# Sample's score items laid over fewer slots of the projection, and six small loads moved from its slot 293 to its slot 287

## What is computed

```python
h = rms_norm(x, ln_w)
proj = einsum('bsd,de->bse', h, w_in)         # 1024 -> 8720 columns: q, k, v of 24 heads, gates, the recurrence's q, k, v
# branch A, three groups of 8 heads, windows 128 / 512 / 2048 with dilation 1 / 4 / 16
s = where(band, q @ k.T, -inf); p = softmax(s); o = p @ v; lse = m + log(den)
o_attn = sum_g softmax_g(lse) * o_g
# branch B, gated linear attention, chunks of 64 (prompt) or 8 (sample)
o_gla, state = gla_recurrence(gq, gk, gv, log_a, s0, chunk)
y = rms_norm(x + (sigmoid(mg_a) * (o_attn * silu(az)) @ w_attn_out
                + sigmoid(mg_b) * (rms_norm(o_gla) * silu(gz)) @ w_gla_out) @ w_out)
```

## Time and profile before

| | us |
|---|---|
| median of 3 runs | 2485.26 (2484.94 to 2485.51) |
| the profiled execution | 2486.58 |
| its span, first to last instruction | 2484.8 |
| TensorE busy in it | 2450.7 (99%) |
| VectorE busy | 1214.5 (49%) |
| ScalarE busy | 908.1 (37%) |
| GpSimd busy | 199.1 (8%) |
| mean granted TensorE clock | 0.996 of full |

### The profile page before, as it was taken

How to read it: one execution, slowest core, us unless ns; L and a number is a source line. 1 busy time by engine, 2 the same in 40 slices (tenths; PEclk the granted TensorE clock), 3 DMA queues, 4 the chain that set the end, 5 groups by cost and what they waited for, 6 DMA issues and landing times.

```text
span 2484.8 us, 37018 instructions
## 1 busy us (share of the span) xinstructions
PE 2450.7 (99%) x13710; PEld 1969.5 (79%) x13710; DVE 1214.5 (49%) x2860; ACT 908.1 (37%) x2163; POOL 199.1 (8%) x367
## 2 busy tenths in 40 slices
PE   9999999999999999999999999999999998999998
PEld 6888887887778888887888888788778755888887
DVE  5323422333321115565666666556756447656663
ACT  5224534443332214223544544445424233212221
POOL 0000000000000000112111111222222100000000
PEclk9999999999999999999999999999999999999999
DMA  6333323332323223457667666797777799444341
GB/s 192 103 121 114 105 91 125 103 100 90 112 96 102 93 91 117 144 170 240 209 220 224 202 204 204 215 296 216 206 230 215 219 338 346 172 161 151 140 167 68
DMA packets 209122, 416.97 MB, mean 168 GB/s; under 512 B 32513, under 2 KB 53521, under 8 KB 206833
## 3 DMA queue, kind: packets, MB, share of 16 engines
q1 hardware_dynamic: 166912, 293.60, 35.5%
q0 software_dynamic: 29712, 95.06, 13.1%
q10 hardware_dynamic: 12320, 25.96, 2.8%
HBM read 313.33 MB, written 112.99 MB: 172 GB/s over the span
## 4 chain that ended last, share of the span: by engine, by line
PE 93%; DMA 3%; DVE 2%; ACT 1%; issue 1%; SPq 0%; POOL 0%; DVEq 0%; ACTq 0%
PE b_acc L1231 20%; PE b_acc L1233 19%; PE b_acc L1232 19%; PE c_p_s L1281 3%; PE c_p_o L1304 3%; PE c_p_t L1292 3%; PE c_p_qk L1268 3%; PE f_p_b L2002 2%; PE f_p_b L2004 2%; PE f_p_b L2003 2%; PE f_p_z L2002 2%; PE f_p_z L2004 2%; PE f_p_z L2003 2%; PE b_acc L1237 2%; PE b_acc L1238 1%; PE e_p_o L1923 1%
## 5 line engine op out<-in xcount | busy, mean ns | idle before, releaser
L1231 PE MATMUL b_acc<-b_whi,hT_hi 128*128 128x512 f32 x2048 | 819.9, 400 | 3.9 <-DVE b_wlo L967 1.5
L1233 PE MATMUL b_acc<-b_whi,hT_lo 128*128 128x512 f32 x2048 | 799.5, 390 | 0.0
L1232 PE MATMUL b_acc<-b_wlo,hT_hi 128*128 128x512 f32 x2048 | 798.6, 390 | 0.0
L1231 PEld LDWEIGHTS b_acc<-b_whi,hT_hi 128*128 128x128 f32 x2048 | 384.4, 188 | 101.2 <-issue 9.8
L1233 PEld LDWEIGHTS b_acc<-b_whi,hT_lo 128*128 128x128 f32 x2048 | 384.5, 188 | 82.4
L1232 PEld LDWEIGHTS b_acc<-b_wlo,hT_hi 128*128 128x128 f32 x2048 | 385.1, 188 | 73.4
L967 DVE SCALAR_TENSOR_TENSOR b_wlo<-b_raw,a_lnw,b_whi 128x512 fp32r<-128x512 f32 x268 | 192.7, 748 | 365.3 <-ACT b_whi L759 364.9
L773 ACT COPY b_stage<-b_acc 128x512 f32<-128x512 f32 (+2 forms) x198 | 115.3, 582 | 539.6 <-PE b_acc L1233 529.4
L797 ACT ACTIVATE c_sm<-c_sm,c_ends 128x256 f32<-128x256 f32 (+1 forms) x384 | 172.8, 451 | 129.9 <-DVE c_ends L1052 129.8
L759 ACT ACTIVATE b_whi<-b_raw,a_lnw 128x512 fp32r<-128x512 f32 x268 | 182.9, 714 | 3.9 <-ACT c_og L815 1.4
L771 ACT ACTIVATE b_stage<-b_acc 128x512 f32<-128x512 f32 x96 | 57.4, 598 | 307.7 <-PE b_acc L1233 307.3
(11 more groups left out here) (320 smaller groups left out, 3091.2 us busy)
## 6 DMA issues: line engine op xcount, KB each, us to landing
b_raw<-in_w_in SPq DMA_DIRECT2D x134, 512.0 KB, 4.3
tm<-b_stage SPq DMA_DIRECT2D x256, 256.0 KB, 2.1
a_x<-tm POOLq DMA_DIRECT2D x192, 256.0 KB, 4.9
b_ck<-in_cache_kv_w POOLq DMA_DIRECT2D x104, 256.0 KB, 5.0
c_qk<-tm SPq DMA_DIRECT2D x101, 256.0 KB, 3.6
f_m<-tm SPq DMA_DIRECT2D x16, 1024.0 KB, 5.8
c_v<-tm SPq DMA_DIRECT2D x53, 256.0 KB, 4.3
og<-c_og ACTq DMA_DIRECT2D x48, 264.0 KB, 3.9
```

The costliest lines, as they stand in the source:

```text
L1231: nc.tensor.matmul(out, stat_hi, mov_hi, start=(k == 0), stop=False)
L1232: nc.tensor.matmul(out, stat_hi, mov_lo, start=False, stop=False)
L1233: return nc.tensor.matmul(out, stat_lo, mov_hi, start=False, stop=(k == KC - 1))
```

## The change

Two lines. In `project`, the items are laid over the slots from begin + 3 to four slots ahead of the last turn's first, instead of six slots ahead of the projection's end: the last item stands in slot 281 instead of 287. In `finish`, SyncE's wait for all scores and the six small loads behind it move from t = 6 to t = 0 of `tile`, from slot 293 to slot 287.

```diff
@@ project
     begin = turns[len(CHUNKS[0])].first
-    item_at = [begin + 3 + m * (NSLOT - 6 - begin - 3) // N_IT for m in range(N_IT)]
+    item_at = [begin + 3 + m * (turns[-1].first - 4 - begin - 3) // N_IT for m in range(N_IT)]
@@ finish, sync, tile(t)
-            if t == TPH - 2:
+            if t == 0:
                 sp.wait_ge(over.scored, over.scores)
                 load_vn(1)
                 sp.dma_start(diag[:, :], A["dec_diag"]).then_inc(gw_in, 16)
                 sp.dma_start(gw[:, :], A["gla_norm_w"].rearrange("a (p b) -> p (a b)", b=1)).then_inc(gw_in, 16)
                 sp.dma_start(g_v[:, :], TMs[SEQ:TOK, TM_GV * CH:(TM_GV + 1) * CH]).then_inc(gw_in, 16)
```

## The result

| | before | after |
|---|---|---|
| median, runs side by side on one chip | 2485.26 us | 2493.25 us |
| lowest to highest | 2483.09 to 2486.06 | 2490.56 to 2494.40 |
| after over before | | 1.0036 [1.0027, 1.0046] |
| span of the profiled execution | 2484.8 us | 2490.8 us |
| mean granted TensorE clock | 0.996 | 0.993 |

The change makes the kernel slower: by 8.0 us between the medians, by 0.36% in the ratio, whose interval lies clear of 1. Forecast were 2484.2 us and a range of 2481.5 to 2488.0. One execution of a kernel further down (the squeezed items) took 6604.77 us, why isn't known, and is left out of that kernel's numbers.

The account below looks back on a forecast made before the run. It took TensorE's matmuls to bound the kernel before 1976 us and the transfer queue from there to 2086 us. Terms 0 + 0 - 1.1 us gave 2484.2 us, from the 2485.26 us median; range 2481.5 to 2488.0.

Parts of the forecast that it names:

- part 1: Score items laid over slots 159 to 281 instead of 159 to 287: cost or gain 0.
- Denser items also mean denser loads: VectorE's waits for score loads, 15.1 us in all, grow five per cent, hidden under matmuls: 0, bounds 0 and +3.9 us.
- the 1.9 us for c_qk: Longest of three TensorE waits from 990 to 1979 us said possibly to concern the change; no term given.
- VectorE's two waits of 1.3 us: TensorE's waits at slot 253's SiLU product and slot 258's recurrence tile: first goes, second grows equally; 0, bounds -2.6 and +2.6.
- rival (d): Faster: both 1.3 us waits go and all 1.4 us of moved loads arrive: -4.0 us, 2481.3 us; chance 0.12.
- Both signs of being wrong: Between 990 and 1979 us, TensorE shows a new wait on VectorE or a new stretch at half clock.
- (b): Last turn: six loads delay the mask up to 1.4 us, TensorE's softmax wait brings half clock: 2489.0 us; chance 0.09.
- (c): Slots 246 to 261: a score-load wait up to 3.9 us reaches TensorE, half clock behind: +6.2, 2491.5 us; chance 0.09.
- Part 2: Six small loads moved to slot 287 fit SyncE's idle 3.7 us, delay nothing, and free the full DMA stretch: -1.1 us.
- The -1.1 us: Gain at V and weight loads after the move, 0.3 us lost to engines running dry; bounds -1.4 and 0.
- the 1.4: Time of all 16 DMA engines for the six loads' 0.49 MB at 353 GB/s, taken out of the full stretch.
- rival (a): The moved loads were hidden anyway, so their 1.4 us is lost where SyncE waits for buffers: 2485.3 us; chance 0.18.

Follow-up runs that it names:

- the squeezed items: The changed kernel with items up to slot 261 placed as before and the last 43 squeezed into slots 262 to 281: 2492.59 us, ratio 1.0027.
- the items alone: The changed kernel with the wait for the scores and the six small loads back in slot 293, items over slots 159 to 281: 2491.84 us, ratio 1.0027.
- GpSimd held back: The changed kernel, with GpSimd waiting for d_glr to land before it issues the loads of item 165: 2486.40 us, ratio 1.0009.
- the loads alone: The kernel before with only the score wait and six small loads moved to slot 287, items where they were: 2483.76 us, ratio 0.9993.
- the 1 MB copy: The kernel before plus a 1 MB memory-to-memory copy issued by SyncE in slot 251, ahead of the recurrence's loads: 2489.44 us, ratio 1.0021.
- the two with both holes: The changed kernel without items in slots 180 to 182 and 250 to 252: 2482.81 us; the same with the small loads back in slot 293: 2485.62 us.
- before with both holes: The kernel before (last item in slot 287, small loads in 293) without items in slots 180 to 182 and 250 to 252: 2489.76 us, ratio 1.0023.
- hole at 180: The changed kernel with no score item in slots 180 to 182 only: 2490.67 us, ratio 1.0028.
- hole at 250: The changed kernel with no score item in slots 250 to 252 only: 2493.30 us, ratio 1.0041.

## Why the prediction was wrong

**The step that failed** is the last paragraph of part 1, "Denser items also mean denser loads", taken at 0. It asked only what a score load does to VectorE, which waits for it, and bounded that by VectorE's waits. It did not ask what the score loads do to the other transfers that are under way. In fact VectorE's waits for them fell (8.6 us in 9 waits, against 15.1 in 11), and the bill came at two of SyncE's loads, for which TensorE waits: 3.9 us at c_qk and 5.9 us at d_glr, wait and half clock together, where the sum had 0. The rows for it were at hand: the 1.9 us for c_qk was named as a wait "that could have to do with this change", and then no step took it up. GpSimd's queue around slots 182 and 252 had to be laid beside SyncE's, item by item by the formula of `item_at`; its gap of 10.13 us ahead of 1738.43 shows how much luck the old list had there.

**Counting items per slot** hid it. 1.67 or 1.76 a slot is a mean; the change shifts the phase of the whole list. The comparison slot by slot was made for VectorE's work at slots 252 to 257, not for the loads, which run up to three items ahead.

**VectorE's two waits of 1.3 us**, sum 0, make -0.7 us in all, within the bounds, but not by the step that was given. The wait for slot 253's product went, as the item count said. The one at the tile of slot 258 was to grow to some 2.6 us; it went too, which was the sign of rival (d). Two others came: 0.5 us for the product of slot 255 and 1.4 us at the tile of slot 276, where before has no wait. The same holds with the items alone and with GpSimd held back. So the number is luck. Both signs of being wrong were fulfilled: a new wait of TensorE on VectorE, and new stretches at half clock. By the formula, slots 282 to 287 lose 10 items, not 11; nothing hangs on it.

**The half clock** was in the text with the right price, half of 6.82 us, but attached to the mask (b) and to a SiLU slot (c), places that it did not touch. In the profiled execution 6.8 us are two such prices. Rival (c) named denser scoring with 2491.5 us, the closest number; its mechanism, a load wait on VectorE that reaches TensorE, is not what happened in the changed kernel. The squeezed one comes near it, at the recurrence's tile, where three load waits and five items stand ahead of it.

**Part 2** held in its places. The six issues and the store behind them, SyncE's queue of after:

```profile
1971.91 1.43 SPq L1727 DMA_DIRECT2D e_vn_b<-tm  x3
...
1974.36 0.47 SPq L1795 DMA_DIRECT2D g_v<-tm  x1
1975.61 0.33 SPq L516 DMA_DIRECT2D tm<-b_stage  x1
```

Less the 8.1 us by which everything is late there, that is 1963.8 to 1966.7 and 1967.5: the issues stand where they were put, and the store is not held. The last score starts at 1929.2, that is 1921.1 without the 8.1 us, against the forecast 1925; it was met by far. Rival (b) is out: VectorE's wait for the mask fell from 4.78 to 3.20 us and TensorE's behind it, for the softmax, from 2.3 to 0.7. That fall isn't part 2's (0.3 us with the items alone, 1.9 with the loads alone), nor does it follow both parts (2.1 us with GpSimd held back, which has them; 0.2 with the 1 MB copy, which has neither); what makes it stays open.

**The -1.1 us** is met in part. Three pairs of kernels differ by part 2 alone: before and the loads alone, the items alone and after, and the two with both holes. The first w_raw landed 65.8 and 65.2 us behind the copy of slot 293 in the first pair, 66.1 and 65.3 in the second, 66.0 and 65.3 in the third, so 0.6 to 0.8 us of the 1.4 arrive there. From that copy to the end the pairs gain 0.7, 2.3 and 2.5 us. In the last two the kernel without the move waits 3.0 us for a split of weights (line 2435 of before), the one with it 0.4 and nothing. But before waits only 1.3 us there, and before with both holes, without the move, is as quick behind the copy (479.4 us) as the kernels with it (479.5 to 480.2). So a gain above 0.8 us isn't shown. The medians (-1.1 us, interval -4.0 to +0.5) can't tell any of it from nothing, nor can the pair with both holes (2482.81 with the moved loads, 2485.62 without, whose intervals overlap). Between the forecast's step and rival (a) it is a draw.

The 8 us in short: 3.9 at c_qk and 5.9 at d_glr, given back in part by smaller waits for VectorE and, in the profiled execution, by a shorter half clock near 434 us, which differs between executions anyway. That the score loads cause both is shown by taking each place away alone. That it is the share of the DMA engines, rather than another limit of the two queues, is argued and not shown: it rests on the shares of queue 0 and on the 1 MB copy, which makes d_glr late without more loads of GpSimd, though in part by a later issue.

## What to carry to other kernels

When a periodic list of work is re-spread, don't compare its density but its phase: lay its transfers beside every small load of the other queues for which the busiest engine waits soon after, and every item beside the due steps of its own engine. A wait that has no half clock behind it today, such as the 1.9 us for c_qk, is the first place to look, because a microsecond more there may cost four. And keep such moments free on purpose: three empty slots at each of the two places took back the 8 us, but a hole pushes its items onto a neighbour, so each new list has to be measured as a whole.

## What the hardware showed

- **A small wait can cost more than double.** At c_qk and d_glr, waits of TensorE of 1.9 us and less had no half clock behind them, those of 2.6 us and more all had, for 3.41 us (2.6, 3.4 and 4.2 us) or 6.83 us (2.7, 2.9, 3.7 and 4.7 us). Elsewhere the border is less plain: the softmax wait in the last turn was followed by 3.41 us at half clock where it took 1.9 us (loads alone) and 2.1 us (hole at 180, GpSimd held back), and by none where it took 2.3 us (before) and 2.1 us (squeezed); at the recurrence's tiles 2.6 us (hole at 250) and 3.4 us (before, both holes) had 3.41 us behind them, the 3.0 us with the hole at 180 none. Nor is the price of one and the same wait fixed: the 2.5 us near 433 us were followed by 6.83 us in before, by 3.41 in after, and by none in the two kernels with both holes and the last item in slot 281.
- **Two queues share the engines unevenly.** With GpSimd's queue at 77.5% of the engines, two loads of 64 KB needed 3.7 and 5.2 us instead of 1.9 and 2.1, the engines moving 318 GB/s in all from 1732 to 1736 us; the 256 KB score loads beside them took 5.3 and 5.6 us.
- **Equal spans, unequal profiles.** The two kernels with both holes and the last item in slot 281 both have spans of 2480.5 us, and medians of 2482.81 and 2485.62. The spans are equal by chance. Up to slot 158 both are the same program, and there the one without the moved loads is 2.4 us ahead of the other; behind slot 293 it loses 2.5 us. What differs between executions without any change of the program is of the size of what is looked for here, which is why places were compared, not totals alone.
